# Finer first loads, compact S5 tables, matmuls on zeros, a spread final norm and x casts ahead of splits and squares in a ten-stage transformer kernel

## The reference

```python
def rms_norm(x, g):
    xf = x.astype(jnp.float32)
    y = xf * lax.rsqrt(jnp.mean(xf * xf, axis=-1, keepdims=True) + EPS)
    return (y * g.astype(jnp.float32)).astype(x.dtype)

def swiglu(h, w_gate, w_up, w_down):
    return (jax.nn.silu(h @ w_gate) * (h @ w_up)) @ w_down

# first_block, per layer
    h = h + MACARON_WEIGHT * swiglu(rms_norm(h, ffn_norm[layer, 0]), ...)
    h = h + (s5_mixer or moba_mixer)(rms_norm(h, mix_norm[layer]), ...)
    h = h + MACARON_WEIGHT * swiglu(rms_norm(h, ffn_norm[layer, 1]), ...)
# second_block, per layer
    h = h + (two attentions side by side, or latent attention)(rms_norm_2(h, ...))
    h = h + jnp.square(jax.nn.relu(hn @ mlp_w1[layer])) @ mlp_w2[layer]
return rms_norm_2(h, final_norm_g)

# s5_mixer: lam = exp(a * dt), coefficients from lam, a, b; a scan over the tokens
    mag = jnp.exp(a_re * dt)
    lam_re = mag * jnp.cos(a_im * dt)
    lam_im = mag * jnp.sin(a_im * dt)
    bb_re, bb_im = cmul(coef_re[..., None], coef_im[..., None], b_re, b_im)
```

## Time and profile before

| | |
|---|---|
| median of 3 runs | 1662.07 us (1661.84 to 1668.64) |
| the profiled execution's own time | 1657.95 us |
| its span, first to last instruction | 1656.2 us |
| busy PE | 1571.1 us (95%) |
| busy DVE | 1098.0 us (66%) |
| busy ACT | 761.3 us (46%) |
| busy POOL | 460.5 us (28%) |
| mean granted PE clock | 0.968 |

### The profile page before, as it was taken

One profiled execution on the slowest core, in us unless ns is written; L12 is line 12 of the kernel. 1 busy time (PEld: TensorE's weight loads), 2 busy tenths in 40 slices (PEclk: granted clock), 3 DMA queues, 4 the chain that ended last, 5 costly groups with the idle time before them and its releaser, 6 DMA issues.

```text
span 1656.2 us, 31321 instructions
## 1 busy us (share of the span) xinstructions
PE 1571.1 (95%) x13050; PEld 1505.9 (91%) x13050; DVE 1098.0 (66%) x1067; ACT 761.3 (46%) x995; POOL 460.5 (28%) x413
## 2 busy tenths in 40 slices
PE   5989998899999999999899999999999998999997
PEld 4989997699999999999889999976999996699996
DVE  7798869957555665566566555645766675476665
ACT  5334360055444544447654343655544455654432
POOL 6999617701000100007540000565100023510000
PEclk8999997699999999999999999999999997999998
DMA  6535540045555465554425555450555542045552
GB/s 214 200 127 203 205 151 26 1 153 176 206 185 195 168 226 184 200 190 166 154 101 182 203 181 201 152 191 1 176 209 186 192 178 77 27 170 211 183 199 76
DMA packets 39027, 265.97 MB, mean 161 GB/s; under 512 B 4352, under 2 KB 6400, under 8 KB 7328
## 3 DMA queue, kind: packets, MB, share of 16 engines
q1 hardware_dynamic: 37808, 261.41, 44.6%
q0 software_dynamic: 1136, 3.38, 0.7%
HBM read 263.70 MB, written 1.06 MB: 160 GB/s over the span
## 4 chain that ended last, share of the span: by engine, by line
PE 83%; DVE 11%; issue 2%; ACT 2%; POOL 2%; DMA 1%; DVEq 0%; SPq 0%; ACTq 0%; POOLq 0%
PE ps L554 77%; DVE gst L1501 3%; PE ps L855 2%; PE ps L845 2%; DVE xlo L1319 2%; DVE wlo L1313 2%; PE ps L833 1%; DVE h L1329 1%; DVE t L1475 1%; DVE t L1476 1%; DMA h<-in_xT 1%; POOL pm L418 1%; PE ps L791 0%; ACT pm L1230 0%; POOL rinv L417 0%
## 5 line engine op out<-in xcount | busy, mean ns | idle before, releaser
L1313 DVE TENSOR_TENSOR wlo<-raw,whi 128x2048 fp32r<-128x2048 f32 x246 | 596.4, 2428 | 220.7 <-ACT whi L995 220.3
L554 PE MATMUL ps<-xhi,whi 128*128 128x256 f32 x2048 | 572.9, 280 | 20.9 <-DVE xlo L1319 13.4
L995 ACT CAST whi<-raw 128x2048 fp32r<-128x2048 f32 x246 | 470.2, 1913 | 243.1 <-PE ps L554 243.0
L554 PE MATMUL ps<-xlo,whi 128*128 128x256 f32 x2048 | 569.6, 278 | 0.0
L554 PE MATMUL ps<-xhi,wlo 128*128 128x256 f32 x2048 | 569.4, 278 | 0.0
L554 PEld LDWEIGHTS ps<-xhi,whi 128*128 128x128 f32 x2048 | 387.8, 189 | 23.9 <-issue 13.4
L554 PEld LDWEIGHTS ps<-xlo,whi 128*128 128x128 f32 x2048 | 388.6, 190 | 0.0
L554 PEld LDWEIGHTS ps<-xhi,wlo 128*128 128x128 f32 x2048 | 387.8, 189 | 0.0
L554 PE MATMUL ps<-hhi,whi 128*128 128x256 f32 x1216 | 335.9, 276 | 0.0
L554 PE MATMUL ps<-hlo,whi 128*128 128x256 f32 x1216 | 335.9, 276 | 0.0
L554 PE MATMUL ps<-hhi,wlo 128*128 128x256 f32 x1216 | 335.9, 276 | 0.0
(11 more groups left out here) (235 smaller groups left out, 2066.8 us busy)
## 6 DMA issues: line engine op xcount, KB each, us to landing
raw<-in_wstream SPq DMA_DIRECT2D x247, 1024.0 KB, 4.8
h<-in_xT SPq DMA_DIRECT2D x1, 1024.0 KB, 8.5
out_hT<-h SPq DMA_DIRECT2D x2, 512.0 KB, 3.0
biasA<-bias_rows POOLq DMA_DIRECT2D x5, 192.0 KB, 5.3
biasB<-bias_rows POOLq DMA_DIRECT2D x3, 192.0 KB, 7.1
braw<-in_s5b POOLq DMA_DIRECT2D x1, 512.0 KB, 4.0
CL<-in_s5c POOLq DMA_DIRECT2D x4, 128.0 KB, 4.3
tg<-in_tgain POOLq DMA_DIRECT2D x1, 384.0 KB, 5.0
```

Source lines behind the costliest of these rows:

```text
L554: return pe.matmul(o, l, r, start=first, stop=last, skip_group_check=True)
L995: act.copy(whi[:, slot, :], raw[:, slot, :]).then_inc(S("whi_ready"), 1)
L1313: dve.tensor_tensor(wlo[:, slot, :], raw[:, slot, :], whi[:, slot, :], ALU.subtract)\
```

## The change

It does six things. First, the start: chunks 0 and 1 are loaded, split and used in halves, x is loaded in four pairs, only the gains are loaded ahead of it, and S5's small operations are put in other places (angles between the splits of chunks 2 and 3, coefficients behind the first hidden tile). Second, PE runs 14 matmuls of 512 columns on one row of zeros before ffn0. Third, POOL's S5 tables are made in pieces of at most 512 elements, B and C in compact form (16 columns), C's second factor too, and ACT copies ("spreads") them into `LB` and `CL` in 16 activations in ffn0's last double iteration, which is taken out of the loop. Fourth, in ffn and mlp stages the next split comes behind all x tiles on DVE, and all squares behind all casts on ACT; behind the out-projections of s5 and moba each pair's squares follow its casts. Fifth, the final norm: gains applied by ACT, sums shorter on DVE, six matmuls, four wide scalings. Sixth, the output is stored in three pieces.

The diff, cut to its core:

```diff
-        zrow = sb("zrow", [1, 64], BF16)
+        zrow = sb("zrow", [1, 512], BF16)
...
-            load(0, None, 0)
-            sp.dma_start(par[:, :], params).then_inc(S("par_loaded"), 16)
-            sp.dma_start(h[:, :, :], xT.rearrange("(k p) t -> p k t", p=P)).then_inc(S("x_loaded"), 16)
-            for n in range(1, NSLOT):
-                load(n, None, n)
+            def load_half(n, half):
+                c = slice(half * CH // 2, (half + 1) * CH // 2)
+                sp.dma_start(raw[:, n, c], wstream[n][:, c])\
+                    .then_inc(S(f"half_landed{n}" if half == 0 else f"raw_landed{n}"), 16)
+            def load_x(b):
+                t = slice(2 * b, 2 * b + 2)
+                sp.dma_start(h[:, t, :], xT.rearrange("(k p) t -> p k t", p=P)[:, t, :]).then_inc(S(f"x_loaded{b}"), 16)
+            load_half(0, 0)
+            sp.dma_start(par[:, 0:C_SD], params[:, 0:C_SD]).then_inc(S("gains_loaded"), 16)
+            load_x(0)
+            load_x(1)
+            load_half(0, 1)
+            load_x(2)
+            load_x(3)
+            load_half(1, 0)
+            load_half(1, 1)
+            sp.dma_start(par[:, C_SD:C_END], params[:, C_SD:C_END]).then_inc(S("par_loaded"), 16)
+            load(2, None, 2)
...
+            for pairs in ((0, 2), (2, 3), (3, 4)):
+                t = slice(2 * pairs[0], 2 * pairs[1])
+                sp.wait_ge(S("out_ready"), pairs[1])
                 sp.dma_start(out.rearrange("(k p) t -> p k t", p=P)[:, t, :], h[:, t, :]).then_inc(S("out_stored"), 16)
-            sp.wait_ge(S("out_stored"), 32)
+            sp.wait_ge(S("out_stored"), 48)
...
+            chain(pool.memset(LB[:, :, :, :, :], 0.0))
+            chain(pool.memset(CL[:, :, :, :, :], 0.0))
...
+                rows = min(NP_S5, 512 // max(w, 1))
+                for q0 in range(0, NP_S5 if w > 0 else 0, rows):
+                    q = slice(q0, q0 + rows)
+                    cm = Ec[:, q, m:m + 1].to_broadcast([P, rows, w])
...
+            def times(dst, src, re, im, sem):
+                c = Q[re].unsqueeze(2).to_broadcast([P, NP_S5, 16])
+                d = Q[im].unsqueeze(2).to_broadcast([P, NP_S5, 16])
+                for r, op in ((0, ALU.subtract), (1, ALU.add)):
+                    chain(pool.tensor_tensor(dst[:, r], src[:, r], c, ALU.mult))
+                    chain(pool.tensor_tensor(ctmp[:, :, :], src[:, 1 - r], d, ALU.mult))
+                    chain(pool.tensor_tensor(dst[:, r], dst[:, r], ctmp[:, :, :], op))
+                pool.nop().then_inc(S(sem), 1)
...
-                ci = Q["ci"][rows].unsqueeze(2).to_broadcast([64, NP_S5, 16])
-                for (r, x, y, op) in ((0, 0, 1, ALU.subtract), (1, 1, 0, ALU.add)):
-                    o = LB[rows, r, 1, :, cols]
-                    chain(pool.tensor_tensor(o, braw[rows, x], cr, ALU.mult))
-                    chain(pool.tensor_tensor(btmp[rows], braw[rows, y], ci, ALU.mult))
-                    chain(pool.tensor_tensor(o, o, btmp[rows], op))
...
+            times(bbar, braw, "cr", "ci", "s5_bbar")
+            times(bturn, bbar, "lr", "li", "s5_bturn")
+            pool.wait_ge(S("c_loaded"), 16)
+            times(cturn, craw, "lr", "li", "s5_cturn")
+            pool.memset(K0[:, :, :], 0.0).then_inc(S("s5_prepared"), 1)
...
-                chunk_ready(n, None)
+                if n < 2:
+                    pe.wait_ge(S("half_low"), n + 1)
+                else:
+                    chunk_ready(n, None)
                 for k in range(KT):
-                    pe.wait_ge(*wait_k(k))
+                    if n < 2 and k == KT // 2:
+                        chunk_ready(n, None)
+                    if wait_k:
+                        pe.wait_ge(*wait_k(k))
...
+                if F == 0:
+                    proj_first(F + 1, 5, None)
+                else:
+                    proj(F + 1, None, 5)
...
+                pe.wait_ge(S("s5_spread"), 16)
...
+            pe.wait_ge(S("ones_set"), 2)
+            for _ in range(14):
+                mm(ps[:, 4, :], zrow[0:1, 0:P], zrow[0:1, :], True, True)
...
-            for n, j in enumerate((0, 1, 6, 7)):
-                if j == 6:
-                    pe.wait_ge(S("final_sq"), 4)
-                last = mm(ps[:, 7, 0:T], ones[:, :], sq[:, j, :], n == 0, n == 3)
+            pe.wait_ge(S("final_sums"), 2)
+            for n, j in enumerate((0, 1, 4, 5, 6, 7)):
+                if j in (4, 6):
+                    pe.wait_ge(S("final_sq"), j // 2 + 1)
+                last = mm(ps[:, 7, 0:T], ones[:, :], sq[:, j, :], n == 0, n == 5)
...
+            def x_high(k, before_last=lambda: None, squares_after="pair"):
...
                 for b in range(4):
                     if b == 3:
                         before_last()
-                    if k:
-                        act.wait_ge(S("h_ready"), 4 * (k - 1) + b + 1)
-                    if b == 3:
+                    act.wait_ge(S("h_ready"), 4 * (k - 1) + b + 1)
+                    if b == 3 and squares_after == "before":
                         squares(b)
                     for j in (2 * b, 2 * b + 1):
                         act.activation(xhi[:, j, :], h[:, j, :], ACT.Copy, scale=gain(k, j)).then_inc(S("xhi_ready"), 1)
-                    if b < 3:
+                    if squares_after == "pair" or squares_after == "before" and b < 3:
+                        squares(b)
+                if squares_after == "all":
+                    for b in range(4):
                         squares(b)
...
-                x_high(NORM_OF[st] + 1, before_last=lambda: split_hi(F + 5))
+                x_high(NORM_OF[st] + 1, before_last=lambda: split_hi(F + 5),
+                       squares_after="before" if st in ("ab", "mla") else "pair")
...
+            def spread(dst, src, scale=1.0):
+                for g in range(2):
+                    rows = slice(64 * g, 64 * g + 64)
+                    act.activation(dst[rows, :, 16 * g:16 * g + 16], src[rows], ACT.Copy, scale=scale)\
+                        .then_inc(S("s5_spread"), 1)
+            def spread_b():
+                act.wait_ge(S("s5_bbar"), 1)
+                for r in range(2):
+                    spread(LB[:, r, 1], bbar[:, r])
+                act.wait_ge(S("s5_bturn"), 1)
+                for r in range(2):
+                    spread(LB[:, r, 0], bturn[:, r])
+            def spread_c():
+                act.wait_ge(S("c_loaded"), 16)
+                act.wait_ge(S("s5_cturn"), 1)
+                for r, sign in ((0, 1.0), (1, -1.0)):
+                    spread(CL[:, r, 0], craw[:, r], sign)
+                    spread(CL[:, r, 1], cturn[:, r], sign)
...
-                split_hi(F + 2)
-                root(NORM_OF[st])
-                split_hi(F + 3)
+                if F:
+                    split_hi(F + 2)
+                    root(NORM_OF[st])
+                    split_hi(F + 3)
+                else:
+                    root(0)
...
+                        if after:
+                            after[u]()
                 body(None)
-                with act.Fori(1, (FFN_IT - 1) // 2) as i:
+                last = (FFN_IT - 1) // 2 - 1
+                with act.Fori(1, last + (1 if F else 0)) as i:
                     body(i)
+                if F == 0:
+                    body(last, after=(spread_b, spread_c))
                 split_hi(F + 3 * FFN_IT + 1)
-                x_high(NORM_OF[st] + 1)
+                x_high(NORM_OF[st] + 1, squares_after="all")
...
+            first_high(0)
+            act.wait_ge(S("gains_loaded"), 16)
+            cast_x(0)
+            cast_x(1)
+            squares(0)
+            squares(1)
+            second_high(0)
+            cast_x(2)
+            cast_x(3)
+            squares(2)
+            first_high(1)
+            squares(3)
+            second_high(1)
+            act.wait_ge(S("par_loaded"), 16)
+            act.activation(Q["dt"], log_dt, ACT.Exp).then_inc(S("s5_dt"), 1)
+            split_hi(2)
+            act.wait_ge(S("s5_x"), 1)
+            act.activation(Q["mag"], Q["x"], ACT.Exp).then_inc(S("s5_mag"), 1)
+            act.wait_ge(S("s5_red"), 1)
+            act.activation(Q["s"], Q["r"], ACT.Sin).then_inc(S("s5_sin"), 1)
+            act.activation(Q["sh"], Q["r"], ACT.Sin, scale=0.5).then_inc(S("s5_sin"), 1)
+            split_hi(3)
...
+            def with_gain(j):
+                act.activation(h[:, j, :], h[:, j, :], ACT.Copy, scale=gain(10, j)).then_inc(S("final_gain"), 1)
             for b in range(4):
                 act.wait_ge(S("h_ready"), 36 + b + 1)
                 act.activation(sq[:, 2 * b:2 * b + 2, :], h[:, 2 * b:2 * b + 2, :], ACT.Square)\
                     .then_inc(S("final_sq"), 1)
+                if b in (1, 2):
+                    act.wait_ge(S("final_sq"), b)
+                    with_gain(2 * b - 2)
+                    with_gain(2 * b - 1)
+            act.wait_ge(S("final_sq"), 4)
+            for j in (4, 5, 6):
+                with_gain(j)
```

(58 more changed lines are left out.)

118 lines of the change are left out of this document (37 added, 81 removed).

## The result

The changed kernel takes 1666.67 us (median; 1664.50 to 1673.89), the kernel before 1659.95 on the same chips (1655.35 to 1668.64). The ratio is 1.0049, 95% interval 1.0036 to 1.0062: about 8 us slower (6.7 by the medians), where 1.7 us faster had been forecast. The time lies inside the range, but not on the side that the forecast had. The profiled run has a span of 1664.9 us against 1656.2.

What follows compares the result with a forecast made beforehand. The matmul engine PE was taken to bound the kernel, with 83% of the span. ffn0 -22.7, end -4.4 and borders +25.4 sum to -1.7, so 1660.4 us from 1662.07; range 1634 to 1673.

Steps and rivals of the forecast that it cites:

- Beginning of ffn0: First feed-forward stage: PE's real work begins near 7.1 us, and its seventh chunk at about 48.0 instead of 59.93, 11.9 us won.
- Stall of ffn0: Later ffn0: tables cut to 512 elements remove the POOL and DVE stall and the low clock behind it, 8.9 us won.
- Rival C: ffn0's end: POOL is late for the spreads, so ACT, DVE and PE wait; +10 to +25, 1670 to 1685 us, chance 0.14.
- Pace of ffn0: ffn0 from the seventh chunk: matmuls 0.1133 us apart once the 7.84 us idling gap closes, 1.9 us won.
- End: Final norm and store: statistics 3.3, scalings 0.5 and last transfer about 0.6 us shorter, 4.4 won in all.
- The wait at the borders: Moba, ab and mla: late squares and POOL's additions start the statistics matmul at 16.2 instead of 11.8, 4.4 us lost each.
- The clock behind the wait: Moba, ab and mla: low clock for 5 us after PE's idling, 2.4 us more lost at each.
- The s5 border: Before s5: spreads delay casts some 1 us, statistics at 17 instead of 13.5, then low clock; 5.9 us lost.
- ffn2: Border in front of ffn2: a second chunk hides the additions, statistics at 16.3 instead of 17.2, 0.9 us won.
- The five borders: Borders behind the ffn stages and first mlp: +25.4 us in sum, bounds -10.5 and +32.
- D: ffn0: the settling matmul again leaves PE at the 0.1177 pace, so ffn0 gains only 17.0; 1666 us, chance 0.04.
- A: Borders partly hidden: POOL adds before DVE's second split and the clock stays up; +5.2 there, 1640.2 us, chance 0.27.

Runs made afterwards that it cites:

- e10: The kernel of e5 without the 14 matmuls on zeros at the start: 1639.38 us, ratio 0.9862 to the kernel before.
- e7: The changed kernel with the whole border as before and POOL's table operations over all 32 rows again: 1648.11 us, ratio 0.9929.
- e4: The kernel before with only the new border (squares behind all casts, split behind the low tiles): 1688.48 us, ratio 1.0180.
- e12: The kernel of e5 with the final norm and output store as before the change: 1640.77 us, ratio 0.9877.
- e1: The changed kernel with squares back between the casts at the ffn and mlp0 borders, split still behind the low tiles: 1642.05 us, ratio 0.9904.
- e8: The changed kernel with PE's second chunk ahead of the statistics matmul in moba, ab and mla: 1651.68 us, ratio 0.9955.
- e9: The changed kernel with PE's idle time before the statistics of moba, ab and mla filled by 54 full-size matmuls: 1657.70 us, ratio 0.9976.
- e5: The changed kernel with the border as before and the eight C spreads moved behind s5's fourth weight split: 1636.27 us, ratio 0.9859.
- e13: The changed kernel, new border kept, with only the eight C spreads moved behind s5's fourth weight split: 1663.27 us, ratio 1.0035.
- e14: The kernel of e1 with the C spreads moved as in e5: 1635.90 us, ratio 0.9862.

## Why the prediction was wrong, point by point

- **Beginning of ffn0: right.** Two chunks done at 21.4 (forecast 20.5), waits of 2.1 and 0.9 (1.8 and 2), the seventh chunk at 48.59 (48.0). Wrong in it: "at full clock from 7 us". The first matmuls came 0.21 apart, and e10 shows no worth of the zeros; it cost little, because x was late anyway.
- **Stall of ffn0: right.** No stall, last matmul at 195.49 (near 195), and e7 confirms the cause. Rival C did not happen, but it was closer than forecast: POOL ended the second of B's two products at 174.31 (168 forecast), and ACT's copies of it begin at 175.53.
- **Pace of ffn0: right in the number, wrong in the reason.** From 50 us on matmuls came 0.1133 apart, which gave the 1.9 us. The reason given was the 7.84 us of idling in front of the settling matmul. But e4 has the same 7.84 and passes 532 matmuls in 45 to 105, and e7, without such idling, passes 512 in 50 to 110, the slow pace (windows of e4, then e7). What sets the pace is open; that it came was luck.

```profile
45.00:105.00 60.00, 60.00 (x532) 60.00 (x531) 48.16 (x24) 20.58 (x16) 58.04 (x26) 1.00 0.51 185
50.00:110.00 60.00, 60.00 (x512) 60.00 (x511) 45.31 (x26) 21.00 (x16) 57.73 (x30) 1.00 0.58 207
```

- **End: right, 0.7 too large.** -3.7 for -4.4, and e12's profile agrees. The statistics gave 3.2 (3.3 forecast), the scalings 0.8 (0.5), but the smaller last transfer gave nothing: 3.7 us behind the last scaling, where it was 3.4 and 0.6 less had been taken.
- **The wait at the borders: right.** Statistics 16.0 after the first addition (16.2), idle 6.50 (6.7). e1 shows that the place of the squares decides, and e8 that the wait costs only because of PE's order.
- **The clock behind the wait: the step that failed.** "24 matmuls pass for 5.1 instead of 2.7: 2.4 more", once at each of three borders, 7.2 in all. That was read off one stall inside ffn0, where the clock was low for 5 us behind the wait and full afterwards. Behind the waits of 6.50 it was low for 6.9 us at moba (until 748.9), 7.2 at ab and 25 at mla (PE busy 19.9 of them). From the kernel before to the changed one the three stretches behind the statistics grew by 13.2. The runs put 9 to 12 of that down to the clock (e9 by medians and by ratios), and the means of the traces 11.5: 2 to 5 more than the 7.2 of the sum. The rest of the 13.2 is not assigned.
- **The s5 border: mis-sized.** Forecast were +3.5 up to its statistics matmul and +2.4 of low clock behind it. Measured: +6.6 and +2.9. The spreads were taken to begin at 188, to last 0.53 each and to delay the casts by 1 us. They began at 190.33 and took 0.65 each from one to the next (a square of 512 elements takes 0.63), 5.2 us for eight; a cast of weights stood behind them, and the third addition to h waited for the casts of x. e5 and e13 put 4.9 and 4.0 down to them.
- **Together.** Over the forecast are s5 by 3.7, the three borders by 5.5 (behind the statistics +6.0, the wait -0.4), ffn0 by 0.9, the end by 0.7, ffn2 by -0.3: 10.5 us, from -1.7 to +8.8. The five borders cost 34.3 where 25.4 had been forecast and +32 was the upper bound.
- **Rivals.** D's 1666 us was the time that came, but its mechanism did not: the pace was 0.1133. A fails in both its conditions: only two of POOL's five additions got in ahead of DVE's second split, and the clock did fall. The 0.14 for "slower" was too small: the forecast lay 1.7 us from no change, and the price of the clock had one row behind it.

The best kernel here is e5, equal to e14: beginning, tables and end as changed, border as before, C spreads behind the border. It takes 0.9859 of the time before, 23 us less.
